# Four quarters of the array and shared bank pairs in the second block's chunked recurrence

## The chip, the cores and the metric

The kernel runs on one core of a Trainium2 chip. The metric is the device time of one execution, in microseconds (us). Everything is fp32.

## The reference, cut to what matters

The program is one block of a first kind followed by two layers of a second kind, over 1024 tokens (the second kind adds 256 context tokens). The change touches only the recurrence of the second kind, an RWKV-7 scan with 6 heads of 64 channels, run forwards and backwards:

```python
def _rwkv7_step(S, inp):
    r, w, k, v, kk, b = inp
    sa = jnp.einsum('bhvk,bhk->bhv', S, kk)
    S = S * w[:, :, None, :] - sa[..., None] * b[:, :, None, :] + v[..., None] * k[:, :, None, :]
    return S, jnp.einsum('bhvk,bhk->bhv', S, r)

    S_f, y_f = lax.scan(_rwkv7_step, S0_f, (r, decay[:, :, 0], kd[:, :, 0], v, kk, bd[:, :, 0]))
    S_b, y_b = lax.scan(_rwkv7_step, S0_b, (r, decay[:, :, 1], kd[:, :, 1], v, kk, bd[:, :, 1]),
                        reverse=True)
```

Chunked over 128 tokens, the corrections `sa` inside a chunk solve a triangular system. With A the strictly triangular product of Q (the kk side) and B (the b side), the kernel needs the inverse of I + A for each head and direction.

## The kernel before, in words

The class `Rwkv` is a stage that has the core to itself. It runs once in each of the two layers, with NCH = 10 chunks of 128 tokens. A chunk has 12 heads-and-directions: direction d (2), tile j of 128 channels (3) and parity p, the head's half of the 128 partitions. `pairs` are the six (d, j), index i below. The five inputs R, Q, K, B, V lie as channels by tokens, so that a head's channels are 64 partitions.

The order of the work is written out by hand. `order(n)` lists the products of step n; the list `prod` over all n is the order in which TensorE makes them. Each product has a place in it, and `bank` gives it PSUM bank place modulo 8, 384 columns wide. `start` waits until the product eight places earlier has been evacuated. `on_act` says which of ACT (`run_act`) and DVE (`run_dve`) evacuates a product; both work through the same list in its order. Step n makes, for chunk n, the inverse and the score matrices, and for chunk n - 1 the state part, interleaved:

- A, AT, E: the triangle's two diagonal 64x64 blocks, the same turned, and the block off the diagonal. For each parity p the row half of the array is p and the column half is the block h; A and AT thus use all four 64x64 quarters and put each parity in a bank of its own.
- Levels 1 to 5 (`y`, `x`, `xT`, for p = 0 then p = 1): Y = M X, X = X - XT' Y, XT = XT - Y' XT. M is AT masked to one level, made by GpSimd (POOL). Block h lies in row half h and goes to column half h, so two quarters of the array, (0,0) and (1,1), work. Y is copied by ACT, X and XT are subtracted on DVE. The results of level 5 go into the full inverse F.
- y6 and z join the two diagonal blocks through E (12 matmuls each).
- QK, RK, RB: 128x128 scores, 64 rows by 128 columns of weights, masked on DVE. t: six groups of three transposes that turn V, K, B.
- State part: G = Q'Hc + QK'V (12 matmuls with 64x128 weights and 12 with 128x128), U = F'G (12 with 128x128), H = K'V + B'U (24 with 128x64), O0 and O1, the output of each direction (18 matmuls each). Hc is H times the decay `fc`.

A matmul in fp32 stands in the trace as two passes, each with its weight load. A chunk has 576 matmuls and 18 transposes. All matmuls of `run_pe` go through the helper `mm` and have line L3294; transposes have L3432.

POOL adds the identity to X (`I`) and XT (`IT`) and makes the masks `M1` to `M5`, each 384 wide for one parity; in step 0 it also clears F and makes `fc`. The SP queue first issues the next stage's loads (`next_loads`), then in step n loads K, B, V of chunk n + 1 after the transposes of chunk n - 1, Q after G, R after O1, and stores the outputs.

A few matmuls of a level, as they stand:

```python
out = start(f"y{l}_{p}@{n}")
for i in range(6):
    for h in range(2):
        ins = mm(out[HALF[h], 64 * i:64 * i + 64], sq(f"M{l % 2}_{p}", h, i), sq(f"X{p}", h, i))
```

Of the kernel before, what the change touches and what calls it, by code (L numbers as in the profile page):

```python
# [3129 lines left out]
class Rwkv(Stage):  # L3130

    def __init__(self, core, rw, fac, y, areas, ready, skip=0):
# [6 lines left out]
        sizes += [(f"t{x}{d}", 384) for d in range(2) for x in "VKB"]  # L3142
        sizes += [(f"{x}{d}{p}", 384) for x in ("QK", "RK", "RB") for d in range(2) for p in range(2)]
        sizes += [(f"F{p}", 768) for p in range(2)]
        sizes += [(f"{x}{p}", 384) for x in ("X", "XT", "AT", "E", "Y", "M0_", "M1_", "G", "U") for p in range(2)]
        sizes += [("H", 384), ("Hc", 384), ("O0", 384), ("O1", 384)]
# [7 lines left out]
        self.prod = [p for n in range(NCH + 1) for p in self.order(n)]  # L3154
        self.place = {p: i for i, p in enumerate(self.prod)}
        on_act = lambda p: p[0] in "yztEGUO" or p[:2] == "AT"
        self.on_act = {p: on_act(p) for p in self.prod}
# [7 lines left out]
        self.s_act = Steps(core.act, [p for p in self.prod if self.on_act[p]], 1)  # L3165
        dve = ["Hc@0"]
        for n in range(NCH + 1):
            for p in self.order(n):
                if not self.on_act[p]:
                    dve.append(p)  # L3170
                if p == f"A1@{n}":
                    dve += [f"XN{i}@{n}" for i in range(2)]
                if p == f"xT3_1@{n}" and n:
                    dve.append(f"Hc@{n}")
        self.s_dve = Steps(core.dve, dve, 1)
        chunk = ["I0", "M1_0", "I1", "M1_1", "IT0", "IT1"], [f"M{l}_{p}" for l in range(2, 6) for p in range(2)]
        self.s_pool = Steps(core.pool, [f"{x}@{n}" for n in range(NCH) for part in (chunk[0], ["F", "fc"] if n == 0 else [], chunk[1])
                                        for x in part], 1)

    def order(self, n):  # L3180

        i, s = n < NCH, n > 0
        out = [f"{x}{p}" for x in ("A", "AT", "E") for p in range(2) if i]
        out += ["G0", "G1"] if s else []
        state = {1: ["U0", "U1"], 2: ["H", "O0"], 3: ["O1"]} if n > self.skip else {1: ["U0", "U1"], 2: ["H"]}
        for l in range(1, 6):
            out += [f"y{l}_{p}" for p in range(2) if i]
            out += state.get(l, []) if s else []
            if i:
                out += [f"{x}{l}_{p}" for p in range(2) for x in ("x", "xT")]  # L3190
                kind = {4: "QK", 5: "RK" if n >= self.skip else None}.get(l)
                out += [f"{kind}{d}{p}" for d in range(2) for p in range(2)] if kind else []
        if i:
            out += ["y6_0", "y6_1"] + [f"RB{d}{p}" for d in range(2) for p in range(2) if n >= self.skip] + ["z0", "z1"]
            out += [f"t{x}{d}" for d in range(2) for x in "VKB"]
        return [f"{p}@{n}" for p in out]

    def bank(self, p):
        return self.c.psum[:, self.place[p] % self.nb, 0:384]
# [18 lines left out]
    def sp(self, sp):  # L3218
# [3 lines left out]
        for n in range(NCH + 1):  # L3222
            if n + 1 < NCH:
                if n > 0:
                    sp.wait_ge(E.sem, E.at(0, f"tB1@{n - 1}"))
                self.load(sp, n + 1, "KBV", 0)
                if n > 0:
                    sp.wait_ge(E.sem, E.at(0, f"G1@{n}"))
                self.load(sp, n + 1, "Q", 1)
                if n > self.skip:  # L3230
                    sp.wait_ge(E.sem, E.at(0, f"O1@{n}"))
                if n + 1 >= self.skip:
                    self.load(sp, n + 1, "R", 2)
            if n > self.skip:
                for d in range(2):
                    sp.wait_ge(A.sem, A.at(0, f"O{d}@{n}"))
                    dst = self.y[d].rearrange("(j p) t -> p j t", p=P)[:, :, (n - 1) * P:n * P]
                    sp.dma_start(dst, tri(self.b[f"O{d}"])).then_inc(self.c.w_in[6].sem, 16)
        sp.wait_ge(self.c.w_in[6].sem, self.out_base + 32 * (NCH - self.skip))

    def run_pool(self, pool):
        b, s, E, A, Dv = self.b, self.s_pool, self.s_pe, self.s_act, self.s_dve
        ident, lev = six(self.c.const("ident64")), lambda l: six(self.c.const("levT64", l))
        for n in range(NCH):
            for p in range(2):
                pool.wait_ge(Dv.sem, Dv.at(0, f"A{p}@{n}"))
                pool.tensor_tensor(hex6(b[f"X{p}"]), hex6(b[f"X{p}"]), ident, ALU.add).then_inc(s.sem, 1)
                if n:
                    pool.wait_ge(E.sem, E.at(0, f"y5_{p}@{n - 1}"))
                pool.wait_ge(A.sem, A.at(0, f"AT{p}@{n}"))  # L3250
                pool.tensor_tensor(hex6(b[f"M1_{p}"]), hex6(b[f"AT{p}"]), lev(1), ALU.mult).then_inc(s.sem, 1)
            for p in range(2):
                pool.wait_ge(Dv.sem, Dv.at(0, f"XN{p}@{n}"))
                pool.tensor_tensor(hex6(b[f"XT{p}"]), hex6(b[f"XT{p}"]), ident, ALU.add).then_inc(s.sem, 1)
            if n == 0:
# [21 lines left out]
    def run_pe(self, pe):  # L3277
# [18 lines left out]
        for n in range(NCH + 1):  # L3296
# [80 lines left out]
            for l in range(1, 6):  # L3377
# [12 lines left out]
                if n > 0 and l < 4:  # L3390
                    state(l)
# [771 lines left out]
```

## Time and profile before

| | |
|---|---|
| median of 3 runs | 4786.05 us (4780.19 to 4786.14) |
| the profiled execution, span of the core | 4776.3 us |
| median less that span | 9.75 us |
| recurrence, first layer | 2252.7 to 2731.5 us of the span |
| recurrence, second layer | 3795.1 to 4273.8 us of the span |
| TensorE busy, whole span | 94% |
| DVE, ACT, POOL busy | 56%, 31%, 20% |

The page gives for each engine the time in which an instruction ran. The profiled execution has no time of its own beside its span; what lies around it is the difference to the runs. Rows by windows give the busy time of TensorE in stretches that can be laid where one product ends and the next begins. Rows by line give the mean duration of one instruction.

### The profile page before, as it was taken

What the parts mean: (1) busy time and instruction counts of PE and PEld (TensorE: products, weight loads), DVE (VectorE), ACT (ScalarE), POOL (GpSimd) and SP (SyncE); (2) the same over time, 40 slices, a digit from 0 to 9 for tenths busy, and PEclk for the clock granted to TensorE, in tenths of its full rate; (3) what the DMA queues carried; (4) which work ended last, traced back from release to release, by engine and by line L of the source; (5) the groups of instructions that cost most, each with busy time, mean ns of one, the idle gap of its engine ahead of it and who ended that gap; (6) DMA issues with size and microseconds to landing.
All of it is one profiled execution on the core that took longest, in us unless ns stands there. A gap on an engine that the chain in (4) does not pass through costs nothing. (4 is left out here: it accounts for less than half of the span.)

```text
span 4776.3 us, 96349 instructions
## 1 busy us (share of the span) xinstructions
PE 4507.4 (94%) x40786; PEld 2851.9 (60%) x40786; DVE 2689.7 (56%) x4592; ACT 1466.0 (31%) x2452; POOL 972.5 (20%) x1169
## 2 busy tenths in 40 slices
PE   9998989899999999999999988999999899989998
PEld 4446855444444445554999855654444499976663
DVE  5754476785432236765545467566676545446656
ACT  2212453100000113332223255543333232326552
POOL 0002211000100000001232243530000132314460
PEclk9998999999999999999999999999999999989999
DMA  4331012443425544444222110323444411111122
GB/s 140 104 100 64 33 63 76 135 139 115 167 71 177 180 139 151 141 166 149 56 58 57 41 56 12 97 71 108 145 157 167 145 49 50 56 33 50 56 69 84
DMA packets 341466, 468.66 MB, mean 98 GB/s; under 512 B 39560, under 2 KB 244648, under 8 KB 340081
## 3 DMA queue, kind: packets, MB, share of 16 engines
q1 hardware_dynamic: 289216, 266.26, 17.8%
q0 software_dynamic: 51824, 196.24, 11.6%
q8 instruction: 328, 5.37, 0.5%
q14 instruction: 98, 0.79, 0.1%
HBM read 328.14 MB, written 147.86 MB: 100 GB/s over the span
## 5 line engine op out<-in xcount | busy, mean ns | idle before, releaser
L491 PE MATMUL psum<-arena 128*128 128x512 f32 x2352 | 1031.2, 594 | 17.6 <-issue 8.0
L3294 PE MATMUL psum<-arena 64*64 64x64 f32 (+6 forms) x22800 | 892.1, 231 | 22.8 <-POOLq L222 7.4
L3294 PEld LDWEIGHTS psum<-arena 64*64 64x64 f32 (+3 forms) x22800 | 853.0, 143 | 64.0 <-issue 22.3
L491 PEld LDWEIGHTS psum<-arena 128*128 128x128 f32 x2352 | 445.6, 190 | 564.7 <-issue 546.1
L1079 PE MATMUL psum<-arena 128*128 128x512 f32 x1344 | 583.8, 595 | 11.6 <-DVEq L222 5.3
L706 PE MATMUL psum<-arena 128*128 128x512 f32 x1232 | 537.0, 596 | 4.8 <-DVE arena L772 2.7
L2677 DVE CUSTOM_DVE_ANT_0 arena<-psum,arena 128x512 f32<-128x512 f32 (+3 forms) x532 | 292.6, 588 | 291.2 <-PE psum L2564 285.9
L1079 PEld LDWEIGHTS psum<-arena 128*128 128x128 f32 x1344 | 254.8, 191 | 330.9 <-issue 320.3
L706 PEld LDWEIGHTS psum<-arena 128*128 128x128 f32 x1232 | 232.6, 190 | 302.5 <-issue 292.4
L3499 DVE TENSOR_TENSOR arena<-arena,psum 128x384 f32<-128x384 f32 x320 | 177.9, 556 | 325.9 <-PE psum L3294 292.6
L2564 PE MATMUL psum<-arena 64*128 64x512 f32 (+3 forms) x1192 | 269.7, 537 | 84.0 <-DVE arena L2677 68.6
L2642 ACT COPY arena<-psum 128x512 f32<-128x512 f32 (+3 forms) x532 | 244.8, 512 | 301.9 <-PE psum L2615 296.0
L2534 POOL TENSOR_TENSOR arena<-arena 128x512 f32<-128x512 f32 (+2 forms) x192 | 222.9, 1171 | 441.0 <-ACT arena L2642 440.8
L2615 PEld LDWEIGHTS psum<-arena 128*128 128x128 f32 x1736 | 187.9, 142 | 146.2 <-issue 114.0
L2648 ACT ACTIVATE arena<-arena 128x1280 f32<-128x1280 f32 (+5 forms) x244 | 256.8, 1066 | 22.2 <-DVEq L2698 22.1
L2580 PE MATMUL psum<-arena 128*64 128x128 f32 x3472 | 252.1, 282 | 8.1 <-DVE arena L2692 8.1
L2615 PE MATMUL psum<-arena 128*128 128x128 f32 x1736 | 253.1, 284 | 5.7 <-ACT arena L2642 5.2
L2580 PEld LDWEIGHTS psum<-arena 128*64 128x64 f32 x3472 | 187.9, 137 | 53.3 <-issue 34.5
L3456 ACT COPY arena<-psum 128x384 f32<-128x384 f32 x200 | 96.1, 481 | 329.2 <-PE psum L3294 329.2
L2564 PEld LDWEIGHTS psum<-arena 64*128 64x128 f32 x1192 | 98.0, 191 | 153.8 <-DVE arena L2677 97.1
L3274 POOL TENSOR_TENSOR arena<-arena 128x384 f32<-128x384 f32 x160 | 155.2, 997 | 162.6 <-PE psum L3294 162.6
L1151 DVE TENSOR_TENSOR arena<-arena,psum 128x512 f32<-128x512 f32 x85 | 57.5, 688 | 183.3 <-PE psum L1079 153.1
(346 smaller groups left out, 5197.5 us busy)
## 6 DMA issues: line engine op xcount, KB each, us to landing
arena<-w_in SPq DMA_DIRECT2D x86, 512.0 KB, 5.6
proj<-arena SPq DMA_DIRECT2D x172, 256.0 KB, 2.0
arena<-w_mod POOLq DMA_DIRECT2D x24, 1024.0 KB, 5.6
arena<-down_sum SPq DMA_DIRECT2D x40, 512.0 KB, 3.7
arena<-proj POOLq DMA_DIRECT2D x31, 640.0 KB, 5.0
arena<-proj SPq DMA_DIRECT2D x28, 640.0 KB, 6.9
arena<-w_down SPq DMA_DIRECT2D x30, 512.0 KB, 3.6
x_home<-arena POOLq DMA_DIRECT2D x26, 512.0 KB, 4.9
```

What stands on the lines that cost most here:

```text
L491: ins = pe.matmul(ps[:, b, :], L[:, k, :], R[:, k, :], start=(p in ("P1", "P5", "P6", "P7") and k == 0), stop=(k == KT // 2 - 1), skip_gro ...
L706: ins = pe.matmul(self.c.psum[:, b, :], L[:, k, :], R[:, k, :], start=(begins and k == 0), stop=(k == KT // 2 - 1), skip_group_check=True)
L1079: ins = pe.matmul(self.bank(j, b), self.left(p, j, left, *g)[:, k - g[0], :], R[:, k - k0, :], start=(x in ("P1", "P5", "P6", "P7") and k ...
L2534: ins = pool.tensor_tensor(t[:, 0:m], x[:, 0:m], x[:, 512:512 + m], ALU.add)
L2564: ins = pe.matmul(ps[:, j, at:at + m], self.q[HALF[j], self.slot(it), q * P:(q + 1) * P], self.k[HALF[j], self.slot(it), k0:k0 + m], start ...
L2580: pe.matmul(ps[HALF[j], bank, 0:P], self.vT[:, it % 2, tiles[c] * P + 64 * j:tiles[c] * P + 64 * j + 64], self.pt[n % 2][j][:, c * P:(c + ...
L2615: ins = pe.transpose(out[:, x:x + P], self.p[n % 3][j][:, at + x:at + x + P], ident)
L2642: act.copy(self.pt[n % 2][j][:, at:at + w], ps[:, 2 + j, 0:w]).then_inc(A.sem, 1)
L2648: act.activation(self.p[x][g][:, 0:wide], self.p[x][g][:, 0:wide], ACT.Exp, bias=low, scale=-1.0).then_inc(A.sem, 1)
L2677: dve.tensor_tensor_reduce(self.p[x][j][:, at:at + w], ps[:, j, 0:w], add, -1.0, 3e38, ALU.add, ALU.min, self.acc[:, 2 * x + j, g:g + 1]). ...
L3294: return pe.matmul(out, lhsT, rhs, start=first, stop=last, skip_group_check=not (first and last))
L3499: dve.tensor_tensor(dst, dst, ps, ALU.subtract).then_inc(s.sem, 1)
```

## The change

The two parities p share one product of 768 columns (12 blocks of 64) in a pair of banks, `bank` = [:, 2i:2i+2, 0:384] with i = place modulo 4, parity or direction in the second index; `start` waits for the product four places back. Buffers, POOL's operations and the evacuations become 768 wide.

In a level, Y = I - M X now (the subtraction from the identity in DVE's evacuation of y), X = XT' Y and XT = Y' XT; ACT copies x, DVE copies xT. For parity 1 the blocks of X, AT, and M lie turned (block h in row half 1 - h), so that y and x go over all four quarters; xT of levels 1 to 4 stays on (0,0) and (1,1), that of level 5 goes over four. A product AU makes parity 1 of the triangle once more, unturned, and DVE makes XT from it (`XP` from AT for parity 0).

Where weights had 128 columns against 64 moving ones (G, U), they go as two halves of 64 columns. y6 uses two quarters, z four. A, AT, AU, E of chunk n + 1 are made in step n after level 4 (a step -1 makes those of chunk 0), X, XT, AT, E have two buffers. QK0 and QK1 move to levels 1 and 2, H to 3, O (both directions) to 4, RB0 and RB1 before and after y6, the transposes (three groups of six) before z.

```diff
-        self.nb = 8
-        sizes += [(f"{x}{p}", 384) for x in ("X", "XT", "AT", "E", "Y", "M0_", "M1_", "G", "U") for p in range(2)]
+        sizes += [(f"{x}{s}", 768) for x in ("X", "XT", "AT", "E") for s in range(2)]
+        sizes += [(x, 768) for x in ("Y", "M0", "M1", "G", "U", "O")] + [("H", 384), ("Hc", 384)]
...
+    def on_act(self, p):
+        n = p.split("@")[0]
+        return n in ("AT", "E", "G", "U", "O", "y6", "z") or n[0] == "t" or (n[0] == "x" and n[1] != "T")
...
+        inv, state, ahead, rows = 0 <= n < NCH, n > 0, n + 1 < NCH, n >= self.skip
...
+        out = mine("y1") + past("G") + mine("x1 xT1 QK0 y2") + past("U") + mine("x2 xT2 QK1 y3") + past("H", inv)
+        out += mine("x3 xT3 y4") + past("O", n > self.skip) + mine("x4 xT4")
+        out += [f"{x}@{n + 1}" for x in ("A", "AT", "AU", "E")] if ahead else []
+        return out + mine("y5") + mine("RK0 RK1", rows) + mine("x5 xT5") + mine("RB0", rows) + mine("y6") + mine("RB1", rows) + mine("tV tK tB z")
...
-        return self.c.psum[:, self.place[p] % self.nb, 0:384]
+        i = self.place[p] % 4
+        return self.c.psum[:, 2 * i:2 * i + 2, 0:384]
...
+        for n in range(-1, NCH):
+            for l in range(2, 6) if n >= 0 else ():
+                if l > 2 or n:
+                    pool.wait_ge(E.sem, E.at(0, f"y{l - 2}@{n}" if l > 2 else f"y4@{n - 1}"))
+                pool.tensor_tensor(flat12(b[f"M{l % 2}"]), flat12(b[f"AT{n % 2}"]), lev(l), ALU.mult).then_inc(s.sem, 1)
...
+                pool.wait_ge(Dv.sem, Dv.at(0, f"A@{m}"))
+                pool.tensor_tensor(X, X, ident, ALU.add).then_inc(s.sem, 1)
+                if n >= 0:
+                    pool.wait_ge(E.sem, E.at(0, f"y5@{n}"))
+                pool.wait_ge(A.sem, A.at(0, f"AT@{m}"))
+                pool.tensor_tensor(flat12(b["M1"]), flat12(b[f"AT{m % 2}"]), lev(1), ALU.mult).then_inc(s.sem, 1)
+                pool.wait_ge(Dv.sem, Dv.at(0, f"AU@{m}"))
+                pool.tensor_tensor(XT, XT, ident, ALU.add).then_inc(s.sem, 1)
...
+            for kind in ("A", "AT"):
+                out = start(f"{kind}@{n}")
...
+                            ins = mm(out[HALF[h ^ p], p, 64 * i:64 * i + 64], tile(l, d, p, j, h), tile(r, d, p, j, h))
...
+            again, off = start(f"AU@{n}"), start(f"E@{n}")
...
+                for h in range(2):
+                    turned = mm(again[HALF[h], 1, 64 * i:64 * i + 64], tile(l, d, 1, j, h), tile(r, d, 1, j, h))
+                    ins = mm(off[HALF[h], h, 64 * i:64 * i + 64], tile(l, d, h, j, 0), tile(r, d, h, j, 1))
...
+        def inverse_y(n, l):
...
+            for i in range(6):
+                for h, p in ((0, 0), (0, 1), (1, 1), (1, 0)):
+                    ins = mm(out[HALF[h], p, 64 * i:64 * i + 64], sq(f"M{l % 2}", h ^ p, p, i), sq(f"X{n % 2}", h ^ p, p, i))
...
+            for kind, lhs, rhs in (("x", XT, "Y"), ("xT", "Y", XT)):
+                out = start(f"{kind}{l}@{n}")
+                for i in range(6):
                     for p in range(2):
+                        for h in range(2):
+                            f = h if kind == "xT" and l < 5 else h ^ p
+                            ins = mm(out[HALF[f], p, 64 * i:64 * i + 64], sq(lhs, h, p, i), sq(rhs, h, p, i))
...
+        def state_g(n):
...
+            for i, (d, j) in enumerate(pairs):
+                for c in range(2):
                     for p in range(2):
+                        mm(out[HALF[c ^ p], p, 64 * i:64 * i + 64], head("Q", d, p, j, n)[:, HALF[c]], sq("Hc", p, 0, i),
+                           first=(i == 0), last=False)
+            for i, (d, j) in enumerate(pairs):
+                for c, p in ((0, 0), (0, 1), (1, 1), (1, 0)):
+                    ins = mm(out[HALF[c ^ p], p, 64 * i:64 * i + 64], mat("QK", d, p, j)[:, HALF[c]], val("V", d, p, j),
+                             first=False, last=(i == 5))
...
+        def state_u(n):
...
+            for p in range(2):
+                for i in range(6):
+                    for c in range(2):
+                        ins = mm(out[HALF[c], p, 64 * i:64 * i + 64], full(p)[:, i, HALF[c ^ p]], tok("G", p, i))
...
+            elif p == "x5":
...
+                for f in range(2):
+                    act.copy(F[HALF[f], :, 3:6, HALF[f]], ps4[HALF[f], :, 3:6, :])
+                    ins = act.copy(self.part(f"X{n % 2}", f)[HALF[f], 0:192], ps[HALF[f], f, 0:192])
...
+            elif p[0] == "x" or p == "AT":
+                ins = act.copy(both(f"{'X' if p[0] == 'x' else 'AT'}{n % 2}"), ps)
...
+            elif p[0] == "y":
+                ins = dve.tensor_tensor(quad(b["Y"]), over12(ident), ps4, ALU.subtract)
...
+            elif p[0] == "x":
+                ins = dve.tensor_copy(b[f"XT{n % 2}"].rearrange("p (a t) -> p a t", a=2), ps)
```

## Rows read from the trace of the kernel before

**Rows 1.** The page: the span, TensorE's busy time, the recurrence's matmuls.
```profile
span 4776.3 us, 96349 instructions
...
PE 4507.4 (94%) x40786; PEld 2851.9 (60%) x40786; DVE 2689.7 (56%) x4592; ACT 1466.0 (31%) x2452; POOL 972.5 (20%) x1169
...
L3294 PE MATMUL psum<-arena 64*64 64x64 f32 (+6 forms) x22800 | 892.1, 231 | 22.8 <-POOLq L222 7.4
```

**Rows 2.** TensorE by windows, us: stretch, length, busy (passes), granted clock, DMA.
```profile
2252.66:2293.49 40.83, 37.83 (x978) 0.87 0.52 179
2293.49:2340.02 46.53, 46.53 (x1171) 1.00 0.19 54
2714.34:2731.46 17.12, 13.44 (x192) 1.00 0.09 25
...
4251.03:4273.83 22.80, 19.31 (x192) 0.70 0.06 18
```

**Rows 3.** TensorE by windows, chunk 4 of layer one, cut by product.
```profile
2433.11:2434.56 1.45, 1.45 (x97) 1.00 0.17 45
2434.56:2435.35 0.79, 0.79 (x37) 1.00 0.68 183
2435.35:2436.70 1.35, 1.35 (x28) 1.00 0.66 190
2436.70:2439.66 2.96, 2.96 (x28) 1.00 0.85 236
...
2441.20:2444.02 2.82, 2.82 (x28) 1.00 0.41 123
2444.02:2448.37 4.35, 4.35 (x145) 1.00 0.03 6
2448.37:2449.92 1.55, 1.55 (x52) 1.00 0.05 11
2449.92:2452.19 2.27, 2.27 (x40) 1.00 0.00 0
...
2458.67:2465.91 7.24, 7.24 (x242) 1.00 0.40 111
2465.91:2467.45 1.54, 1.54 (x28) 1.00 0.04 11
...
2473.43:2474.97 1.54, 1.54 (x26) 1.00 0.00 0
...
2476.51:2477.52 1.01, 1.01 (x26) 1.00 0.05 16
...
sum 46.54, PE 46.54; mean PE 2.45
```

**Rows 4.** Groups by line and form, whole program: evacuations and POOL, mean ns.
```profile
L3499 DVE TENSOR_TENSOR arena<-arena,psum 128x384 f32<-128x384 f32 x320 | 177.9, 556 | 325.9 <-PE psum L3294 292.6
...
L3274 POOL TENSOR_TENSOR arena<-arena 128x384 f32<-128x384 f32 x160 | 155.2, 997 | 162.6 <-PE psum L3294 162.6
...
L3460 ACT COPY arena<-psum 128x384 f32<-128x384 f32 x236 | 100.7, 494 | 179.3 <-PE psum L3294 177.2 <-PE psum L3432 1.6
...
L2021 POOL TENSOR_TENSOR arena<-arena 128x512 f32<-128x512 f32 x8 | 10.2, 1269 | 19.8 <-PE psum L2040 19.8
...
L3786 DVE TENSOR_TENSOR arena<-psum,arena 128x1024 f32<-128x1024 f32 x8 | 9.8, 1226 | 16.6 <-PE psum L3732 16.6
...
L3609 ACT COPY arena<-psum 128x1024 f32<-128x1024 f32 x6 | 6.1, 1013 | 17.7 <-PE psum L3570 17.7
```

**Rows 5.** Timeline, first layer's tail: U, its evacuation, H.
```profile
2719.06 2.89 PE L3294 MATMUL psum<-arena 128*128 128x64 f32 x24 [0.35 <-ACT arena L3460]
...
2721.99 0.49 ACT L3458 ACTIVATE arena<-psum 128x384 f32<-128x384 f32 x1 [0.85 <-PE psum L3294]
...
2722.53 6.17 PE L3294 MATMUL psum<-arena 128*64 128x64 f32 x120 [0.58 <-ACT arena L3458]
```

**Rows 6.** DMA issues, 2240 to 2740 us: size, median us to landing.
```profile
arena<-rw_V SPq DMA_DIRECT2D x18, 192.0 KB, 3.8
```

More of the change, by code:

```diff
@@ L3164, in __init__ @@
         self.s_pe = Steps(core.pe, self.prod, 1)
-        self.s_act = Steps(core.act, [p for p in self.prod if self.on_act[p]], 1)
+        self.s_act = Steps(core.act, [p for p in self.prod if self.on_act(p)], 1)
         dve = ["Hc@0"]
[L3167 to L3174, printed above, removed]
@@ new lines, in __init__ @@
+        for p in self.prod:
+            if p[:2] == "AU":
+                dve.append("XP" + p[2:])
+            if not self.on_act(p):
+                dve.append(p)
+            if p[:4] == "xT4@" and p != "xT4@0":
+                dve.append("Hc" + p[3:])
+        self.s_dve = Steps(core.dve, dve, 1)
+        pool = []
+        for n in range(-1, NCH):
+            pool += [f"M{l}@{n}" for l in range(2, 6) if n >= 0] + [f"{x}@{n + 1}" for x in ("I", "M1", "IT") if n + 1 < NCH]
+            pool += ["F", "fc"] if n < 0 else []
@@ L3241, in run_pool @@
     def run_pool(self, pool):
         b, s, E, A, Dv = self.b, self.s_pool, self.s_pe, self.s_act, self.s_dve
[L3243 to L3255, printed above, removed]
[L3256 to L3257 removed]
+        ident, lev = twelve(self.c.const("ident64")), lambda l: twelve(self.c.const("levT64", l))
@@ new lines, in scores @@
+        def scores(n, kind, d):
+            l, r = {"QK": "KQ", "RK": "KR", "RB": "BR"}[kind]
+            if kind == "RK" and d == 0:
+                pe.wait_ge(self.c.w_in[3 * (n % 2) + 2].sem, self.in_base[n % 2][2] + 32 * ((n - self.skip) // 2 + 1))
+            out = start(f"{kind}{d}@{n}")
+            for j in range(RT):
+                for p in range(2):
+                    ins = mm(out[:, p, j * P:(j + 1) * P], head(l, d, p, j, n), head(r, d, p, j, n))
+            ins.then_inc(s.sem, 1)
@@ new lines, in state_o @@
+        def state_o(n):
+            pe.wait_ge(A.sem, A.at(0, f"U@{n}"))
+            pe.wait_ge(Dv.sem, Dv.at(0, f"RB1@{n}"))
+            out = start(f"O@{n}")
+            for d in range(2):
+                at = lambda p, j: out[HALF[p], d, j * P:(j + 1) * P]
+                for j in range(RT):
+                    for p in range(2):
+                        mm(at(p, j), sq("Hc", p, 0, d * RT + j), head("R", d, p, j, n), first=(j == 0), last=False)
+                for j in range(RT):
+                    for p in range(2):
+                        mm(at(p, j), val("V", d, p, j), mat("RK", d, p, j), first=False, last=False)
+                for j in range(RT):
+                    for p in range(2):
+                        ins = mm(at(p, j), tok("U", p, d * RT + j), mat("RB", d, p, j), first=False, last=(j == RT - 1))
+            ins.then_inc(s.sem, 1)
@@ new lines, in run_pe @@
+        for n in range(-1, NCH + 1):
+            inv, state, rows = 0 <= n < NCH, n > 0, n >= self.skip
+            for l in range(1, 6):
+                if inv:
+                    inverse_y(n, l)
+                if state and l == 1:
+                    state_g(n - 1)
+                if state and l == 2:
+                    state_u(n - 1)
+                if state and inv and l == 3:
+                    state_h(n - 1)
+                if n > self.skip and l == 4:
+                    state_o(n - 1)
+                if inv and l == 5 and rows:
+                    scores(n, "RK", 0)
+                    scores(n, "RK", 1)
+                if inv:
+                    inverse_x(n, l)
+                if inv and l < 3:
+                    scores(n, "QK", l - 1)
+                if n + 1 < NCH and l == 4:
+                    ahead(n + 1)
+            if inv:
+                if rows:
+                    scores(n, "RB", 0)
+                join(n)
+                if rows:
+                    scores(n, "RB", 1)
+                for x in "VKB":
+                    turn(n, x)
+                joined(n)
```

408 lines of the change are left out of this document (171 added, 237 removed).

## The prediction

> **What bounds the kernel now.** The page's first part is read first: TensorE is busy for 94% of the span [rows 1]. That alone says little, so the stage that the change touches is taken by itself. It runs twice (one layer each). The view by windows, one row for a chunk, shows a later chunk at 46.53 us, all of it TensorE, at a granted clock of 1.00 (the 2.4 GHz level) [rows 2]. The same view cuts one chunk where the kind of product changes [rows 3]: the stretches add to 46.54 us and no other engine is waited for. So a steady chunk costs what its TensorE passes cost. (A matmul in fp32 leaves two passes in the trace; the counts below are two per matmul of the code, and the rows count a few more where a pass crosses a cut.) Only chunk 0 (37.83 of 40.83 us busy, at 0.87) and the tail after chunk 9 (13.44 of 17.12) hold waits [rows 2].
>
> In order, [rows 3] are A with AT, E, G's two halves, U, the x and xT of level 1 with y2, H, O0, levels 3 and 4, QK, y6 and z; y1, level 2, O1, level 5, RK, RB (both as QK) and the transposes are left out. Read by quarter of the array, they give the prices. The triangles put four successive matmuls on four quarters: 96 passes in 1.45 us, 15.1 ns each. A level of the inverse uses two diagonal quarters: 144 in 4.35 and 240 in 7.24, 30.2 ns. y6 uses one: 24 in 1.54, 64 ns. Two 128x64 tiles (H): 48 in 1.55, 32.3 ns. One 128x128 tile (U): 24 in 2.82, 118 ns.
>
> **The change part by part, for a steady chunk.**
> 1. Levels. 5 x (y, x, xT) are 720 passes x 30.2 = 21.8 us. Afterwards y and x of all levels and xT of the fifth go over four quarters, 528 x 15.1 = 8.0; xT1 to xT4 stay on two, 192 x 30.2 = 5.8. Saved: 8.0.
> 2. G. Before 1.35 + 2.96 = 4.31. Afterwards its Q half is 48 passes on four quarters (0.72) and its QK half 48 passes on two 128x64 tiles (1.55). Saved: 2.0.
> 3. U. 24 passes at 118 ns become 48 at 32.3, so 2.82 becomes 1.55. Saved: 1.3.
> 4. y6 goes from one quarter to two (1.54 to 0.73), z from 1.01 to four quarters (24 x 15.1 = 0.36). Saved: 1.5.
> 5. AU is new. With E it makes 48 passes, 24 of them on quarter (1,1), so the y6 row prices the pair: 1.54 in place of 0.79. Cost: 0.8.
> 6. QK and RB are split into single visits. A visit to another tile shape costs 0.1 to 0.3 above its passes (QK: 1.54 for 24 passes, where the 24 of G's first half took 1.35). Two more visits: 0.6. H, O (two of 2.27), the triangles and the transposes keep their passes.
> TensorE therefore needs 46.5 - 8.0 - 2.0 - 1.3 - 1.5 + 0.8 + 0.6 = 35.1 us.
>
> **Hand-offs.** The two head parities no longer take turns, so each level is y, evacuation, x, evacuation, y. A 768-wide DVE evacuation isn't in the trace; it lies between 384 wide (0.556) and 1024 wide (1.226), and the straight line through both gives 0.96. ACT likewise: 0.494 and 1.013 give 0.81 [rows 4]. The tail shows what stands around an evacuation: U's last pass has its 0.22 us to run after issue (the page's mean for a pass of this line is 0.231 [rows 1]), ACT starts 0.04 after it (2721.95 to 2721.99), and H starts 0.05 after ACT (2722.48 to 2722.53) [rows 5]. y to x then takes 0.26 + 0.96 + 0.05 = 1.27 us; its cover is G (2.3), U (1.55), H (1.55), O (4.5) and RK (1.5). x to y takes 1.12, under xT (1.4) and more. At levels 2 and 3 the margin is 0.3, and DVE still has xT and QK of 0.96 each ahead of the y, which use it up without going over. Only y6 is uncovered: x5 is now two wide and two narrow ACT copies, some 1.4 + 0.3 against 0.7 + 0.8 of xT5 and RB0. I take 0.3 us of stall, bounds 0 and 3. If the cover were gone altogether, 10 hand-offs would cost some 12 us.
> Four bank pairs replace eight banks, so a product now waits for the evacuation four back. The tight one is y5 behind A: xT4, Hc and A queue on DVE for 0.96 + 0.56 + 0.96, while TensorE has AT, AU, E (2.2) to do; nothing to 0.3.
> POOL: 384 wide 0.997, 512 wide 1.269 [rows 4], so 768 wide 1.8; seven of them are 12.6 us of 35, each due a level or more later. M1 waits for y5, and IT stands behind it: 3.7 us after y5, due at x1 some 10 us later: hidden. DVE comes to about 18 us, ACT to 13 [rows 4]; neither bounds. XP reads SBUF alone and may share it with POOL; double its 0.55 would still lie under E.
> The SP queue: K, B, V of the next chunk are issued at the chunk's start and land in 3.8 us each [rows 6]. They are now wanted at its level 4, some 20 us in, and only G (Q) and O (R) stand in that queue. Hidden. In chunk 0, whose loads follow the attention's first ones, level 4 comes some 25 us in; bounds 0 and 5 us for each layer.
> So a steady chunk takes 35.4, 11.1 less.
>
> **Sum.** Nine chunks per layer: 100. Chunk 0 has no state part: 8.0 + 1.5 - 0.8 - 0.6 = 8.1 saved in passes. Its waits were 7.5 (40.83 less 46.5 - 4.3 - 2.8 - 1.6 - 4.5); now y1 and x1 wait for three POOL operations of 1.8 in a row (4.3), y2 for M2 behind POOL's set-up (some 3.5), and x2 to x5 have no state work as cover (4 x 1.2): 12.6. So 3 saved. The tail has G, U and O in a row: 2.0 + 1.3 + 1.5 (H dropped) less 1.2 for wider evacuations: 3.6 saved. Per layer 106.6, for two 213. The profiled execution's span is 4776.3 [rows 1], 9.75 under the median of 4786.05; the sum is made on the span and carried over: 4563.3, or **4573 us** as a median.
>
> **A page against this change.** In every product of a level the matmuls of row halves 0 and 1 write the two partition halves of one bank, at 30 ns a pass where y6, in one quarter, takes 64 [rows 3]: they overlap. The sum rests on these rows. The Trainium skill, TensorEngine Tiling (Array Packing), section Restrictions and Gotchas, says that different row tiles cannot access the same PSUM bank at the same time. By that rule the parities that now share bank pairs would run two at a time and the levels would gain nothing; this trace disagrees for halves of a bank, but it has no row with four quarters crossing two banks.
>
> **Rivals.**
> A. Four quarters that cross the two banks don't overlap, so y, x, xT5 and G's Q half keep 30 ns a pass: 576 x 15.1 = 8.7 us a chunk given back, 20 chunks, 174: 4573 + 174 = 4747. For: a quarter's neighbours now write the other bank, which the triangles (each row half in its own bank) never did. Against: the level rows. 4%.
> B. The wide evacuations outrun their cover (1.226 instead of 0.96, say, or more): 0.5 us at 5 to 10 hand-offs, 2.5 to 5 a chunk, 50 to 100 in all: 4623 to 4673. For: margins of 0.3 us. Against: every level has work of other products between. 12%.
> C, slower than before. The granted clock falls to the 1.2 GHz level for part of each chunk once TensorE waits in it, as in chunk 0 (0.87) and in the second layer's tail, whose 192 passes took 19.31 us at 0.70 where the first layer's took 13.44 at 1.00 [rows 2]: time goes with 1/clock. The 35 us of a chunk grow by 35 x (1/c - 1), which is 11.1 at c = 0.76; below that the change loses. At the tail's 0.70 it is 15: 3.9 a chunk over before, 4786 + 78 = 4864. Against: TensorE is left under 1 us of waits in 35. 2%.
>
> **Numbers.** My sum 81%; A 4%, B 12%, C 2%, and 1% that waits of 11 us a chunk leave it level. The range reaches from 4550 (no visit costs, no stalls, U and G's second half at 30.2 in place of 32.3: 0.6 + 0.3 + 0.2 = 1.1 us less, 20 times) to 4635 (stalls of 3 us a chunk more, most of B). Within 0.2% (10 us, what a measurement here can tell) nothing but the last case falls: faster 0.97, same 0.01, slower 0.02.
>
> **What would show it.** Windows of a steady chunk at 35 to 36 us, TensorE busy over 95% of it, at 1.00; y and x as 48 passes in 0.7 us each; 768-wide evacuations at 0.9 to 1.0 on DVE and 0.8 on ACT; U in 1.5, G in 2.3. Wrong if y takes 1.4 (A), if TensorE idles before x or y with DVE as releaser (B), or if the clock is under 0.95 in a steady chunk (C).

## The result, and the profile after the change

The changed kernel takes **4638.98 us** (median of 4 runs, 4637.36 to 4655.24) against 4783.38 for the kernel before on the same chip: ratio 0.9711, 95% interval 0.9696 to 0.9726. It is faster by 144 us; 213 were forecast (4573, range 4550 to 4635), so a third of the gain is missing and the time lies just past the range. The profiled execution took 4639.85 us, its span is 4638.1, so the sum, which was made on the span, compares as 4563.3 forecast against 4638.1: 74.8 us are missing (66 between the medians: the 9.75 us carried over were 0.9 this time, which is luck in the forecast's favour).

The page of the changed kernel, its totals, its instruction queue and the groups of the second recurrence (the matmul helper is now L3299):

```profile
span 4638.1 us, 98695 instructions
...
PE 4306.3 (93%) x42610; PEld 2633.3 (57%) x42610; DVE 2605.2 (56%) x4158; ACT 1445.0 (31%) x2274; POOL 949.7 (20%) x1027
...
q8 instruction: 340, 5.57, 0.5%
...
L3299 PE MATMUL psum<-arena 64*64 64x64 f32 (+4 forms) x24624 | 689.9, 231 | 82.7 <-issue 51.4
L3299 PEld LDWEIGHTS psum<-arena 64*64 64x64 f32 (+2 forms) x24624 | 635.1, 140 | 138.3 <-issue 78.1
...
L3550 DVE COPY arena<-psum 128x768 f32<-128x768 f32 x80 | 76.7, 959 | 296.9 <-PE psum L3299 296.9
...
L3252 POOL TENSOR_TENSOR arena<-arena 128x768 f32<-128x768 f32 x80 | 145.6, 1823 | 257.1 <-PE psum L3299 257.1
```

TensorE is still the busiest engine, but its group now has 82.7 us of idle time ahead of it, 51.4 of it marked "issue": no engine, no semaphore and no data transfer is named as what it waited for. The wide evacuations take what was estimated from [rows 4] (DVE 0.96 us, POOL 1.82).

By windows, TensorE alone (columns as in [rows 2], to which these answer): chunk 0 of the first layer, four later chunks, and the tail with the first matmuls of the next stage (which begins at 2666.33):

```profile
2252.96:2297.34 44.38, 36.32 (x1123) 0.78 0.49 166
2297.34:2336.88 39.54, 36.46 (x1267) 1.00 0.23 63
2336.88:2376.80 39.92, 36.55 (x1267) 1.00 0.23 63
2376.80:2417.38 40.58, 37.08 (x1268) 1.00 0.22 63
2457.19:2498.06 40.87, 37.95 (x1268) 0.96 0.22 62
...
2651.64:2671.00 19.36, 12.65 (x255) 0.84 0.19 62
```

A steady chunk takes some 39.8 us instead of 46.53 [rows 2], where 35.4 were forecast, and 3 us or so of it TensorE is idle, at a granted clock of 1.00. Before, nothing of it was idle.

Is a price wrong? Windows on single products of the chunk that begins at 2376.80, namely x1, y2, U, H and O, answer to [rows 3]:

```profile
2380.57:2381.32 0.75, 0.75 (x52) 1.00 0.94 271
2385.37:2386.23 0.86, 0.86 (x51) 1.00 0.14 38
2386.23:2387.78 1.55, 1.55 (x55) 1.00 0.00 0
2392.61:2394.15 1.54, 1.54 (x53) 1.00 0.04 11
2397.48:2401.97 4.49, 4.49 (x82) 1.00 0.01 4
```

No. x1 and y2 are 48 passes each on four quarters across two banks, in 0.75 and 0.86 with their visit (15.1 ns a pass was forecast), and U is 1.55 us. Cut at fixed counts of passes, the shortest duration of each product over the 14 steady chunks of full length adds up to **35.24 us**; the forecast said 35.1. What is missing is what comes on top: those 14 chunks have a mean of 39.75, so **4.5 us of each are waits**. (They are more than the window's idle time, since short ones vanish under the modelled ends of matmuls.)

Where they lie is seen in the timeline of the same chunk (start, length, engine, line, tile shape, shape, passes, and in brackets the idle time ahead of the piece):

```profile
2376.80 5.97 PE L3299 MATMUL psum<-arena 64*64 64x64 f32 x259
2384.19 7.62 PE L3299 MATMUL psum<-arena 64*64 64x64 f32 x254 [1.42 <-issue]
2392.22 3.32 PE L3299 MATMUL psum<-arena 64*64 64x64 f32 x127 [0.41 <-issue]
2395.79 10.88 PE L3299 MATMUL psum<-arena 64*64 64x64 f32 x381 [0.26 <-issue]
2407.86 3.65 PE L3299 MATMUL psum<-arena 64*64 64x64 f32 x127 [1.19 <-issue]
2411.68 3.65 PE L3299 MATMUL psum<-arena 64*64 64x64 f32 x100 [0.17 <-issue]
```

```profile
2300.00:2600.00 300.00, 278.24 (x9521) 0.99 0.23 64
```

and the instruction queue's row in the view of the DMA queues (packets, MB, share):

```profile
q8 instruction: 75, 1.23, 1.7%
```

The same two rows of the kernel before:

```profile
2300.00:2600.00 300.00, 299.84 (x7546) 1.00 0.18 52
```

```profile
q8 instruction: 60, 0.98, 1.3%
```

A group lasted 5.0 us before and lasts 4.0 now. The trace ties the stops to the packets one by one. The GB/s row of the chunk above, in slices of 1.01 us:

```profile
GB/s 16 179 131 289 267 279 281 117 19 22 0 0 16 0 0 0 16 0 0 16 0 0 0 16 0 7 217 331 236 15 3 16 0 0 0 16 0 0 0 0
```

A slice of 16 is one instruction packet and nothing else. The packets in the 13th and the 17th slice landed at 2390.66 and 2394.37 us by the trace's records of transfers, and TensorE went on at 2392.22 and 2395.79, 1.56 and 1.42 us later. In 2297 to 2617 us there are 30 stops of over 0.15 us, and **every one ends 1.27 to 1.56 us after a packet has landed**; an instant picked at random has a packet that far behind it in 7% of cases. The 51 stops of e11 in the same stretch, with another program, end 1.04 to 1.60 us after a landing.

The **theory** that the runs test: TensorE's instructions arrive one packet at a time, and one group can't on average follow the other faster than every 3.7 to 4 us. Products of the quick kind need less (128 passes at 15.1 ns are 1.9 us), so they run out of instructions. **Rivals**: only the passes count and the waits have another cause; or an added instruction costs its own time and nothing more. The Trainium skill, Runtime: NRT & Kernel Launch, section Instruction fetch mechanics, says that instructions come in blocks of 16 KiB, 256 of them, and that crossing a block boundary costs little and is mostly hidden. On the size this trace agrees (16.4 KB a packet, and 254 counted instructions of TensorE in it); on the cost it disagrees, with 51.4 us ahead of this group's matmuls.

### The profile page after: what moved, and what is told of

The parts are those of the page before. It is cut to its first block and busy times, and to the rows that moved or that the text cites. A ratio compares the mean times of both kernels' runs of the same rounds, so it can differ in the third digit from the quotient of the medians.

```text
span 4638.1 us, 98695 instructions
## 1 busy us (share of the span) xinstructions
PE 4306.3 (93%) x42610; PEld 2633.3 (57%) x42610; DVE 2605.2 (56%) x4158; ACT 1445.0 (31%) x2274; POOL 949.7 (20%) x1027
## 3 DMA queue, kind: packets, MB, share of 16 engines
q8 instruction: 340, 5.57, 0.5%
## 5 line engine op out<-in xcount | busy, mean ns | idle before, releaser
L3299 PE MATMUL psum<-arena 64*64 64x64 f32 (+4 forms) x24624 | 689.9, 231 | 82.7 <-issue 51.4
L3299 PEld LDWEIGHTS psum<-arena 64*64 64x64 f32 (+2 forms) x24624 | 635.1, 140 | 138.3 <-issue 78.1
L3550 DVE COPY arena<-psum 128x768 f32<-128x768 f32 x80 | 76.7, 959 | 296.9 <-PE psum L3299 296.9
L3252 POOL TENSOR_TENSOR arena<-arena 128x768 f32<-128x768 f32 x80 | 145.6, 1823 | 257.1 <-PE psum L3299 257.1
L554 DVE TENSOR_TENSOR arena<-arena 128x512 f32<-128x512 f32 x168 | 115.5, 688 | 52.6 <-PE psum L462 34.2
```

The lines of the kernel that those rows point to most:

```text
L3252: pool.tensor_tensor(flat12(b[f"M{l % 2}"]), flat12(b[f"AT{n % 2}"]), lev(l), ALU.mult).then_inc(s.sem, 1)
L3299: return pe.matmul(out, lhsT, rhs, start=first, stop=last, skip_group_check=not (first and last))
```

## The experiments

All ratios are to the kernel before, run on the same chip in the same series; differences from the changed kernel are differences of these ratios times 4783.

**e1 and e2: empty instructions.**

```diff
+            for _ in range(8):
+                pe.nop()
```

(4 in place of 8 in the kernel before, which has twice as many products.)

> The changed kernel with 8 no-operation instructions put on TensorE's queue ahead of each product of the second recurrence, some 260 in a chunk, about one more group of 256. They move no data and wait for nothing. Supply theory (a group of 256 TensorE instructions can't begin sooner than about 3.9 us after the one before it): a chunk grows by one group, from 39.7 to about 43.6 us, 3.9 x 20 = 78 us in all, the matmuls' own busy time stays at about 36.5 us in a chunk, and the idle pieces marked issue still lie 256 instructions apart, no-operations counted. Rival, that TensorE is held by the work itself and a no-operation only costs its own time on the queue: the same number of no-operations costs the kernel before just as much.

> The kernel before with 4 no-operation instructions ahead of each product of the second recurrence, of which there are twice as many, so again some 260 in a chunk. Supply theory: its 46.5 us for 9.15 groups of 256 are 5.1 us a group, and with 10.2 groups they are 4.6, still over the 3.9, so hardly anything is added: 0 to 15 us in all. Rival, that a no-operation costs its own time on the queue: as much as it costs the changed kernel (some 78 us if that one shows 78).

Both measured as the kernels without them (0.9711 and 0.9997), and the pages show why: 98,695 and 96,349 instructions, not one more than without, and 340 and 328 packets on the instruction queue, also as without. The no-operations never reached the program, so these runs say nothing for or against. They serve as repeats: the changed kernel gives 4640.39 again.

**e3: y, x and xT5 on two quarters.**

```diff
-   sq(f"M{l % 2}", h ^ p, p, i), sq(f"X{n % 2}", h ^ p, p, i)
+   sq(f"M{l % 2}", h, p, i), sq(f"X{n % 2}", h, p, i)
...
-   f = h if kind == "xT" and l < 5 else h ^ p
+   f = h
```

> The changed kernel with y, x and xT5 of the inverse on two quarters of the array again, the instruction count unchanged. The turn of the odd head parity between halves is left out with it, so the values of that parity are not the reference's; shapes, counts, waits and evacuations are the same. Pass theory (the price of a pass decides, as in the forecast): the quartered products lose the -8.0 us of a chunk that the forecast gave them, so some 158 us slower than the changed kernel, 4797. Supply theory: the two-quarter products fill the time that TensorE now idles for its next 256 instructions, so of the 8.0 us only some 4 show: chunk about 43.4 us, 75 to 90 us slower than the changed kernel, 4715 to 4730, and the idle time marked issue of the second recurrence falls from some 4 us in a chunk to under 1.5.

(It leaves out the turn of parity 1 between the halves.) 4742.43 us, ratio 0.9927 (0.9912 to 0.9941): 103 us slower than the changed kernel. The shortest durations add up to 43.21, +8.0 as the prices say, but the chunk grows by 5.2 only, to 44.99, because the waits fall from 4.5 to 1.8 us. Its timeline of one chunk has one stop left, inside the run of quick products A, AT, AU, E:

```profile
2439.93 32.51 PE L3299 MATMUL psum<-arena 64*64 64x64 f32 x1025
2473.41 8.92 PE L3299 MATMUL psum<-arena 64*64 64x64 f32 x223 [0.97 <-issue]
```

The pass theory (158) is out. The supply theory is right in kind, its 75 to 90 too low. Of the 103, 7.7 are in the two chunks 0. So the four quarters were worth 103 us where the forecast counted 8.0 x 20 = 160.

**e4: U by 128-column weights**, 48 instructions fewer.

```diff
-                    for c in range(2):
-                        ins = mm(out[HALF[c], p, 64 * i:64 * i + 64], full(p)[:, i, HALF[c ^ p]], tok("G", p, i))
+                    ins = mm(out[:, p, 64 * i:64 * i + 64], full(p)[:, i, :], tok("G", p, i))
```

(The evacuations of x5, xT5 and z store parity 1's columns of F unturned for it.)

> The changed kernel with U formed by 128-column weights again (12 matmuls in place of 24, 48 instructions of TensorE fewer in a chunk); nothing is left out. Pass theory: the halves of U were priced at -1.3 us in a chunk, so 1.3 x 20 = 26 us slower, 4665. Supply theory: 48 instructions fewer are 0.19 of a group of 256, -0.7 us in a chunk where the group is bound by its supply, and up to +0.6 where U lies in a group that is not: between 14 us faster and 10 us slower.

4667.31 us, ratio 0.9767 (0.9753 to 0.9782): 27 us slower, the pass theory's number and outside what the supply theory allowed. The windows show that the number is a coincidence (three of its steady chunks, the first and the third of them slow):

```profile
2378.16:2424.95 46.79, 42.80 (x1244) 0.89 0.19 54
2424.95:2464.38 39.43, 37.53 (x1243) 1.00 0.23 64
2545.48:2589.14 43.66, 41.00 (x1243) 0.92 0.21 58
```

Three of the 14 steady chunks ran at a granted clock of 0.86 to 0.92, part of their time at the 1.2 GHz level. The other 11 have a mean of 40.5 us, 0.8 over the changed kernel where the passes alone give +1.35; these three are 16 us longer together. The fall follows a long stop: in the first of them TensorE idles for 1.77 us marked issue, and the 127 passes behind it take 8.9 us. So 0.8 x 18 + 16 = 30 us in this execution, of which half is clock. Neither theory had that. Stops of 1.83 and 1.98 us in the same trace were followed by no fall, so whether a given stop costs clock is not shown, nor that e4 loses this much in each execution.

**e5 and e6: added matmuls of one column by one weight column.**

```diff
+            for _ in range(2):
+                pe.matmul(self.bank(p)[0:1, 0, 0:1], ident[0:64, 0:1], ident[0:64, 0:1], start=True, stop=True)
```

(One in place of two in the kernel before.)

> The changed kernel with two matmuls of one column on one weight column put ahead of each product of the second recurrence, into a place of the bank that the product then overwrites: 264 TensorE instructions more in a chunk (2 x 33 products x 4), 1.03 groups of 256. Supply theory (a group can't begin sooner than some 3.7 to 3.9 us after the one before it): +3.8 us in a chunk, 70 to 80 us in all, whatever the added matmuls themselves take; idle pieces marked issue still lie 256 instructions apart, and their sum in a chunk grows. Rival, that only an instruction's own time counts: the same sum as in the kernel before with as many added, and the idle time marked issue stays as it is.

> The kernel before with one such matmul of one column ahead of each of its products, of which it has twice as many: some 260 TensorE instructions more in a chunk, the same as e5. It shows what they cost where groups of 256 take 5.1 us: supply theory, only their own time, 132 passes of 14 to 28 ns, 1.8 to 3.7 us in a chunk, 35 to 70 us in all, with next to no idle time marked issue. The theories differ in the difference between e5 and e6: supply theory says that the changed kernel pays more, by 10 to 40 us; the rival says equal within 5 us.

4759.91 (0.9957, 0.9942 to 0.9972) and 5035.64 us (1.0540, 1.0522 to 1.0557): 118 and 258 us more, where 70 to 80 and 35 to 70 were expected: both missed. The added matmuls are of another tile shape (64x1), and a visit to it costs far more than the 14 to 28 ns a pass that were assumed: 258 / 20 / 65 products = 0.20 us for each product before (2 added passes). In the changed kernel (34 products, 4 added passes each) the shortest durations grow by 8.2 us a chunk, 0.24 for each product, but the chunk by 6.0 only, to 45.74, as the waits fall from 4.5 to 2.3. The two totals, meant to be compared, don't tell the theories apart, since the visits differ in number. The changed kernel alone does: its instructions' own time would give 8.2 x 20 = 165 us. In passing: with every product longer, the idle time marked issue of 2300 to 2600 us fell from 21.6 to 6.0.

**e7: RK0, RK1 between A and AT, AU and E behind y5.**

```diff
-        out += [f"{x}@{n + 1}" for x in ("A", "AT", "AU", "E")] if ahead else []
-        return out + mine("y5") + mine("RK0 RK1", rows) + mine("x5 xT5") + mine("RB0", rows) + mine("y6") + mine("RB1", rows) + mine("tV tK tB z")
+        out += nxt("A") + mine("RK0", rows) + nxt("AT") + mine("RK1", rows) + mine("y5") + nxt("AU E")
+        return out + mine("x5 xT5") + mine("RB0", rows) + mine("y6") + mine("RB1", rows) + mine("tV tK tB z")
```

> The changed kernel with RK0, RK1 (12 slow passes each) moved from behind y5 to between the quick products A and AT of the next chunk, and AU and E moved to between y5 and x5; the same instructions, the same results. Pass theory: no change, within 5 us. Supply theory: the run of quick products A, AT, AU, E (192 passes, 384 instructions, 2.7 us of work, where the longest idle pieces lie) is broken by 1.3 us of work that needs few instructions, so that 0.5 to 1 us in a chunk comes back: 8 to 20 us faster than the changed kernel.

4642.77 us, ratio 0.9713 (0.9698 to 0.9727): no change. The 8 to 20 us expected are absent. They had been guessed, not worked out. After this run the theory was put into numbers: each group of 128 passes (a packet) lasts as long as its passes by their shortest durations, **but at least 3.7 us**. That one number, set so that the changed kernel comes out, gives for this order 39.7 too, where 40.21 was measured. (With groups of 127, as the stops show, the number is 3.67 and the chunks come out the same.) A group holds more than the products that were moved, so their places hardly matter.

**e8: G by 128-column weights**, 96 instructions fewer.

```diff
-                for c in range(2):
-                    for p in range(2):
-                        mm(out[HALF[c ^ p], p, 64 * i:64 * i + 64], head("Q", d, p, j, n)[:, HALF[c]], sq("Hc", p, 0, i),
-                           first=(i == 0), last=False)
+                for p in range(2):
+                    mm(out[:, p, 64 * i:64 * i + 64], head("Q", d, p, j, n), sq("Hc", p, 0, i), first=(i == 0), last=False)
```

(The half with QK in the same way.)

> The changed kernel with G's products formed by 128-column weights again (24 matmuls in place of 48, 96 TensorE instructions fewer in a chunk). The turn of the odd head parity between halves is left out with it, so the values of that parity are not the reference's. By the prices of the passes alone: +2.0 us in a chunk, 40 us slower than the changed kernel. Supply theory: the passes' +2.0 less what 96 instructions fewer, 0.37 of a group, give back of the waits (0.37 x 3.9 = up to 1.4): 0.6 to 2.0 us in a chunk, 12 to 40 us slower, the shortest chunk-wise times of each product adding up to 2.0 more, and the waits on top of them to less than before.

(It leaves out the turn of parity 1 between the halves.) 4656.27 us, ratio 0.9744 (0.9728 to 0.9760): 16 us slower. Shortest durations 37.25 (+2.0, as priced), chunk 40.30 (+0.55), waits 3.05 in place of 4.5. The 96 instructions saved give back 1.5 us, against 0.37 x 3.9 = 1.4 expected. The change to G was worth 16 us, not 40.

**e9 and e10: added matmuls of one column in the product's own tile shape**, 240 instructions a chunk in each kernel.

```diff
+            for q in range(4 if p[0] in "xy" and p[1] != "6" else 0):
+                pe.matmul(self.bank(p)[HALF[q % 2], 0, 0:1], ident[HALF[q % 2], 0:64], ident[HALF[q % 2], 0:1], start=True, stop=True)
```

(2 in place of 4 in the kernel before.)

> The changed kernel with four matmuls of one column ahead of each y, x and xT product, this time on 64x64 weights and alternately on the two quarters with which the product itself begins, so that no tile shape is changed: 60 matmuls, 120 passes, 240 TensorE instructions more in a chunk. A one-number model (each group of 256 TensorE instructions lasts as long as its own work by the shortest times seen for each product, but at least 3.7 us), set by the changed kernel's chunk of 39.75 us, gives chunks of 43.0 to 43.4 us, according to whether an added pass itself takes 14 or 28 ns: +3.2 to +3.7 us in a chunk, 60 to 70 us in all. Rival, only an instruction's own time counts: +1.7 us (14 ns) to +3.4 us (28 ns), the same as in e10.

> The kernel before with two such matmuls ahead of each of its y, x and xT products, of which it has twice as many: the same 240 TensorE instructions more in a chunk. Supply theory: groups of 256 last 4.8 us here, so only the added passes' own time shows, 1.7 to 3.4 us in a chunk, 35 to 65 us in all, and idle time marked issue stays near none. If the added pass's own time is near 14 ns, the changed kernel pays 25 to 30 us more for the same instructions than this one; the rival says the same within 5.

4715.93 (0.9863, 0.9849 to 0.9878; +73 us) and 4844.61 us (1.0137, 1.0120 to 1.0153; +66 us). An added pass turned out at 28 ns (8 of them 0.22 us), which is close to what supply allows (3.7 us / 128 = 29 ns), so both theories give nearly the same. Chunk 43.54 against the model's 43.4, but the pair decides nothing.

**e11: the same on four quarters in turn**, so that an added pass is quick.

```diff
+            for q in range(8 if p[0] in "xy" and p[1] not in "T6" else 0):
+                a, c = (q & 1) ^ (q >> 1 & 1), q & 1
+                pe.matmul(self.bank(p)[HALF[c], a ^ c, 0:1], ident[HALF[a], 0:64], ident[HALF[a], 0:1], start=True, stop=True)
```

> The changed kernel with eight matmuls of one column ahead of each y and x product (not xT), in turn on the four quarters, in the order that the product itself has: 80 matmuls, 160 passes, 320 TensorE instructions more in a chunk, which overlap as the quick products' own do. The theories are told apart by what the same passes themselves take, read as the shortest duration of those products over the chunks less what it was: at 14 to 20 ns a pass that is 2.2 to 3.2 us in a chunk. Supply theory with the one-number model (at least 3.7 us for a group of 256): chunks of 44.0 to 44.2 us in place of 39.75, +4.3 to 4.5 us in a chunk, 80 to 90 us in all, and the waits of a chunk grow from 4.5 to 6 us or more. Rival, only an instruction's own time counts: 45 to 64 us in all, waits unchanged.

4733.77 us, ratio 0.9896 (0.9878 to 0.9913): **88 us slower**, within the 80 to 90, out of the rival's 45 to 64. The 160 added passes take 2.2 us of a chunk themselves (14 ns each), the chunk grows by 4.8 to 44.55, and the waits from 4.5 to 7.1. 2300 to 2600 us by windows, and the instruction queue's row:

```profile
2300.00:2600.00 300.00, 267.12 (x9636) 1.00 0.21 58
```

```profile
q8 instruction: 76, 1.25, 1.7%
```

With 13% more instructions to a chunk, TensorE gets through 9636 passes in 300 us instead of 9521: the rate of instructions hardly moves (+1.2%), the chunk gets longer. Between the two theories this run decides; that the limit is the arrival of instructions, and not another that also counts them, is what the landings above show. 3.7 us is the average that fits and not a floor for single intervals: the shortest between the starts of two packets is 3.22 us in the traces of this study (e12), and in the changed kernel's first recurrence 37 of 98 are under 3.7.

**e12: tV between A and AT, tK between AT and AU.**

```diff
-        out += [f"{x}@{n + 1}" for x in ("A", "AT", "AU", "E")] if ahead else []
+        out += nxt("A") + mine("tV") + nxt("AT") + mine("tK") + nxt("AU E")
...
-                for x in "VKB":
-                    turn(n, x)
+                turn(n, "B")
```

> The changed kernel with two of its three transposed inputs, tV and tK (6 transposes each, the slowest passes of a chunk: 24 instructions in 0.7 us), moved from behind RB1 into the run of quick products, tV between A and AT of the next chunk and tK between AT and AU; the same instructions and results. Pass theory: two more changes of tile shape, so 0 to 8 us slower than the changed kernel. Supply theory with the one-number model (3.7 us for a group of 256): 38.8 in place of 39.9 us for a chunk, -1.1, less up to 0.4 for the tile shapes: 10 to 20 us faster than the changed kernel, 4619 to 4629. The same model gives 39.9 for the order of e7, no change, as was measured.

4637.69 us, ratio 0.9691 (0.9673 to 0.9709): 10 us less by the ratio, 1 by the medians, the interval overlaps that of the changed kernel, and the steady chunk is 39.86 against 39.75. Not shown to be faster, and no version here beats the changed kernel for certain. Two things ate the gain. The shape changes cost 0.74 us (shortest durations 35.98), not 0.4. (Six transposes, 12 instructions, take 0.7 us, so the two moved inputs hold 24 instructions in 1.4 us; the text on record gives the 0.7 for both.) And the waits fell only from 4.5 to 3.9: the 1.1 us ahead of or in AU with E went, but 1.2 came back in G and xT1 of the next chunk, ahead of which the slow transposes had stood. The model gives 39.07 here, 0.8 too little.

The model against the runs of the changed kernel that altered its program (per steady chunk, mean of 14, in us; e5's row was worked out afterwards):

| kernel | TensorE instructions | shortest durations | measured | model, 3.7 |
|---|---|---|---|---|
| changed | 2532 | 35.24 | 39.75 | 39.73 (set) |
| e3 two quarters | 2532 | 43.21 | 44.99 | 44.75 |
| e4 U whole | 2484 | 36.60 | 40.5 (11 at full clock) | 40.62 |
| e5 one-column extras | 2804 | 43.48 | 45.74 | 45.89 |
| e7 order | 2532 | 35.61 | 40.21 | 39.71 |
| e8 G whole | 2436 | 37.25 | 40.30 | 40.69 |
| e9 two-quarter extras | 2772 | 38.54 | 43.54 | 43.36 |
| e11 four-quarter extras | 2852 | 37.44 | 44.55 | 44.00 |
| e12 turns moved | 2532 | 35.98 | 39.86 | 39.07 |

## Why the prediction was wrong

**The passes (right).** "TensorE therefore needs ... 35.1 us": 35.24. Single terms are 0.1 to 0.2 us off and partly cancel (AU with E 1.32 where 1.54 was taken, y6 0.84 for 0.73). The levels' 8.0 is confirmed by e3 (+8.0), U's 1.3 by e4 (+1.35), G's 2.0 by e8 (+2.0).

**Hand-offs (right in kind).** The evacuations cost 0.96 and 0.80 to 0.81 us, and in 2300 to 2600 us no wait of TensorE has DVE, ACT or POOL as releaser. Rival B, the one that was given most, didn't happen. Nor did A (y2 in 0.86 us) or C's loss.

**The step that failed** is the sum's assumption, made in one sentence on [rows 3], that "a steady chunk costs what its TensorE passes cost", with "0.3 us of stall" for hand-offs alone. The sum left out the time in which TensorE's instructions arrive. The assumption holds while a packet of them lasts well over 3.7 us. Before, a packet took 46.5 / 9.2 groups = 5.1 us. At the forecast's own 35.4 us and 10.0 groups, the average is 3.6 us and a run of quick products far less. The runs show in its place a chunk of 39.75 us where 35.4 were forecast, 4.35 more, in waits that end some 1.4 us after a packet of instructions has arrived (the landings) and that grow when quick instructions are added (e11). The change made each instruction shorter and also added 192 to a chunk (2340 to 2532: G, U and AU), and the trace of before had no row in which that resource shows as a wait. What it had were the queue's 328 packets on the page and its packet size, from which 5.1 us a group follows, but not the limit.

**Where the 74.8 us are.** Chunks 1 to 9 of layer one went from 420.85 us (2293.49 to 2714.34) to 354.30 (2297.34 to 2651.64), 66.6 saved against 100: 33.4 missing. In layer two they went from 413.4 to 345.7: 32.3 missing. Together 65.7, in 18 chunks, 61 of it in the 14 of full length. The other 9 us: 6.6 in layer one's chunk 0 and 0.3 in layer two's, 1.2 in layer one's tail and some 6 outside the recurrence, whose cause was not sought; layer two's tail saved 4.5 more than forecast, since the kernel before had run it at a clock of 0.70 [rows 2]. These last terms are the luck of single executions.

**Chunk 0** was forecast at 37.8 and took 44.38 in layer one: 6.6 more. Its waits for evacuations are as priced (1.08 each against 1.2), but two stops for instructions come on top, and the clock. In e1, which is the same program, it took 41.39, so some 3 us of the 6.6 belong to this one execution. The same stretch of the timeline of the changed kernel, and then of e1:

```profile
2274.86 0.57 PE L3299 MATMUL psum<-arena 64*64 64x64 f32 x20 [1.37 <-issue]
2276.48 5.38 PE L3299 MATMUL psum<-arena 64*64 64x64 f32 x144 [1.06 <-DVE arena L3541]
```

```profile
2273.81 0.56 PE L3301 MATMUL psum<-arena 64*64 64x64 f32 x20 [0.39 <-issue]
2275.43 3.02 PE L3301 MATMUL psum<-arena 64*64 64x64 f32 x144 [1.06 <-DVE arena L3543]
```

After 1.37 us of idleness the same 144 passes take 5.38 us, after 0.39 they take 3.02. The granted clock was at its lower level (0.5) from 2275.7 to 2282.5 in the first. So C's mechanism is there, in chunk 0 and in e4, behind some of the stops and not behind others as long; the changed kernel's steady chunks are at 1.00 but for one at 0.96. The tail, up to the next stage's first matmul, went from 17.12 us to 14.7, 2.4 saved of 3.6.

**Where the 3.7 us come from.** At the 30 stops of the changed kernel the interval has three parts (medians): the packet is under way for 1.06 us, TensorE goes on 1.42 us after it has landed, and the next packet starts 1.23 us after that, never under 1.06. They add to 3.7. So at these stops the next packet was never under way while TensorE still waited for this one. Why each part is as long as it is stays open. Whether data transfers lengthen the interval was not tried. In 2297 to 2617 us the 16 packets with data transfers beside them took 0.88 to 1.91 us (median 1.11), and each had a stop behind it; the other 64 took 0.88 to 1.39 (median 0.98), and 14 had one. But the loads lie at fixed places of a chunk, beside the same products each time, so the two causes aren't separated. The model's misses (0.8 us in e12, 0.5 in e7 and e11, 0.4 the other way in e8) are unexplained.

## What to carry to other kernels

Beside the sum of the passes, work out a second one: TensorE instructions (two for each pass here) in groups of 254, each counted as 3.7 us at least (the number that fits this kernel; it was not measured on another); a stretch takes the longer of the two, group by group. Where a change makes instructions shorter or splits one into two, that second sum decides: splitting G into halves took 2.0 us of passes out of a chunk and brought 0.55. A look at the page's instruction queue, and at the number of passes in the pieces between stops marked "issue" (127, 254, 381), tells whether a kernel is there already; moving products about hardly helps once the average is near the limit.

## What the runs showed of the hardware

- TensorE executed no more than 9521 to 9636 passes in 300 us (31 to 32 ns a pass, 4.0 us for a packet of the instruction queue) in the changed kernel, e9 (9548) and e11, with data transfers at some 60 GB/s, though single products run at 15. The changed kernel's stops end 1.27 to 1.56 us after an instruction packet has landed.
- The granted clock fell to its lower level behind some stops of TensorE and not behind others: after one of 1.77 us in e4, 127 passes took 8.9 us, while stops of 1.83 and 1.98 us in the same trace had no fall behind them.
- One-column matmuls on a 64x1 tile between products of 64x64 tiles cost 0.20 us for each visit of two passes (e6) and 0.24 for one of four (e5, by the shortest durations); in the products' own shape an added pass costs 14 ns on four quarters and 28 on two (e11, e9).
